# Gate stage of a two-block transformer kernel: gating products on GpSimd, convolution one tile later, attention steps packed earlier

## The reference

```python
h = rmsnorm(x, norm_mix[0])
proj = h @ a_w_in[0]                       # 3 * 768 + 256 columns
gate_b, gate_c, hv, qm = split(proj)       # 768, 768, 768, 256
u = gate_c * hv
y = w_conv[0]*shift(u,2) + w_conv[1]*shift(u,1) + w_conv[2]*u    # causal, 3 taps
main = gate_b * y
mo = memory_attention(qm, mem_n, ...)      # 4 heads of 64 over 256 memory rows
x = x + concat(main, mo) @ w_o[0]
```

## Time and profile before

| | |
|---|---|
| median of 3 runs | 1888.3 us (1887.41 to 1896.14) |
| profiled execution, its own time | 1887.41 us |
| its span in the profile | 1885.6 us |
| PE busy | 1812.6 us, 96% |
| DVE busy | 955.2 us, 51% |
| ACT busy | 751.8 us, 40% |
| POOL busy | 135.2 us, 7% |
| granted TensorE clock, mean | 0.984 |

### The profile page before, as it was taken

One profiled execution on the slowest core, in us unless ns is written; L12 is line 12 of the kernel. 1 busy time (PEld: TensorE's weight loads), 2 busy tenths in 40 slices (PEclk: granted clock), 3 DMA queues, 4 the chain that ended last, 5 costly groups with the idle time before them and its releaser, 6 DMA issues.

```text
span 1885.6 us, 21605 instructions
## 1 busy us (share of the span) xinstructions
PE 1812.6 (96%) x8477; PEld 1482.7 (79%) x8477; DVE 955.2 (51%) x1696; ACT 751.8 (40%) x1475; POOL 135.2 (7%) x169
## 2 busy tenths in 40 slices
PE   7999999999999999999999999998998799999997
PEld 5887888888887777777888888776787688888885
DVE  5666443434344667755443433599944444244345
ACT  6433342323234556645232323423756343232232
POOL 0000010101001111001010101010110000000000
PEclk9999999999999999999999999999998899999999
DMA  6222233333333111123323333222100233333321
GB/s 232 81 68 82 87 93 98 99 99 97 95 101 83 56 56 57 34 58 88 100 91 101 100 91 100 86 73 67 56 1 11 79 100 101 101 90 101 101 90 56
DMA packets 195748, 158.37 MB, mean 84 GB/s; under 512 B 5248, under 2 KB 161152, under 8 KB 195648
## 3 DMA queue, kind: packets, MB, share of 16 engines
q1 hardware_dynamic: 194240, 154.16, 27.2%
q0 software_dynamic: 400, 1.25, 0.3%
q10 hardware_dynamic: 1008, 1.59, 0.2%
HBM read 154.88 MB, written 2.10 MB: 83 GB/s over the span
## 4 chain that ended last, share of the span: by engine, by line
PE 85%; DVE 10%; ACT 3%; issue 1%; DMA 0%; ACTq 0%; DVEq 0%
PE ps L752 28%; PE ps L754 26%; PE ps L753 26%; DVE sb L2261 3%; DVE sb L1856 1%; PE ps L804 1%; PE ps L1184 1%; DVE sb L2387 1%; DVE sb L1870 0%; PE ps L1072 0%; ACT sb L1403 0%; DVE sb L2392 0%; PE ps L1078 0%; ACT sb L1390 0%; DMA sb<-in_con 0%
## 5 line engine op out<-in xcount | busy, mean ns | idle before, releaser
L752 PE MATMUL ps<-sb,sb 128*128 128x512 f32 (+3 forms) x2547 | 990.6, 391 | 20.3 <-DVE sb L1856 7.6
L754 PE MATMUL ps<-sb,sb 128*128 128x512 f32 (+3 forms) x2547 | 968.0, 382 | 0.0
L753 PE MATMUL ps<-sb,sb 128*128 128x512 f32 (+3 forms) x2547 | 967.8, 382 | 0.0
L752 PEld LDWEIGHTS ps<-sb,sb 128*128 128x128 f32 (+1 forms) x2547 | 479.7, 189 | 129.6 <-issue 19.7
L754 PEld LDWEIGHTS ps<-sb,sb 128*128 128x128 f32 (+1 forms) x2547 | 479.5, 189 | 92.4
L753 PEld LDWEIGHTS ps<-sb,sb 128*128 128x128 f32 (+1 forms) x2547 | 480.3, 190 | 85.7
L1856 DVE TENSOR_TENSOR sb<-sb,sb 128x512 fp32r<-128x512 f32 x532 | 351.1, 701 | 351.8 <-ACT sb L1382 351.0
L1382 ACT ACTIVATE sb<-sb 128x512 fp32r<-128x512 f32 x532 | 305.2, 622 | 432.2 <-PE ps L754 432.2
L2065 DVE TENSOR_TENSOR sb<-sb,sb 128x512 fp32r<-128x512 f32 x64 | 68.1, 1063 | 177.0 <-ACT sb L1525 177.0
L650 POOL TENSOR_TENSOR sb<-sb 128x512 f32<-128x512 f32 x64 | 66.9, 1045 | 793.5 <-ACT sb L1535 793.5
L1535 ACT ACTIVATE sb<-ps 128x512 f32<-128x512 f32 x64 | 38.3, 598 | 208.6 <-PE ps L754 208.6
(11 more groups left out here) (204 smaller groups left out, 1031.9 us busy)
## 6 DMA issues: line engine op xcount, KB each, us to landing
sb<-in_w_up SPq DMA_DIRECT2D x86, 512.0 KB, 3.9
sb<-in_w_down SPq DMA_DIRECT2D x86, 512.0 KB, 3.8
sb<-in_w_gate SPq DMA_DIRECT2D x22, 512.0 KB, 3.8
sb<-in_a_w_in SPq DMA_DIRECT2D x20, 512.0 KB, 3.7
sb<-in_w_in SPq DMA_DIRECT2D x20, 512.0 KB, 3.7
sb<-in_w_o SPq DMA_DIRECT2D x16, 512.0 KB, 3.8
sb<-in_w_mem_kv SPq DMA_DIRECT2D x8, 512.0 KB, 7.1
sb<-in_w_out SPq DMA_DIRECT2D x8, 512.0 KB, 3.9
```

What stands on the lines that cost most here:

```text
L752: mm(ps, lh, rh, start=start, stop=False, **k)
L753: mm(ps, lh, rl, start=False, stop=False, **k)
L754: return mm(ps, ll, rh, start=False, stop=stop, **k)
```

## The change

1. `PLAN_A`: the norms of all queries and keys are packed into slots 0 to 3, the turns kt 0 0 and kt 0 1 share slot 2, qt 0 and qt 1 slot 3, qt 2 and qt 3 slot 4; attention starts at slot 5 instead of 7; the second layer's keys have na in slot 29, nb in slot 30, both turns in slot 31, instead of one step a slot in 28 to 33.
2. `RB2`, the square of the spread row norm, goes; a buffer `U2` comes. VectorE's three evictions of a block are now alike: U1, U2 and G are each `ps * RB`.
3. GpSimd makes `U3 = U1 * U2` and `G = G * Y`. VectorE's multiply `Y * RB` goes.
4. The three convolution instructions move on VectorE from behind tile c = 1 to behind tile c = 2 and behind the steps of slot 2n+1.
5. ScalarE and VectorE split the weights of tile n ahead of slot 2n instead of behind it.
6. `gate_hi` waits for GpSimd's product.

```diff
-    PLAN_A[1] += [("na", "q", 0)]
-    PLAN_A[2] += [("nb", "k", 0, 0), ("nb", "k", 0, 1), ("na", "q", 1)]
-    PLAN_A[3] += [("kt", 0, 0), ("nb", "q", 0), ("na", "q", 2)]
-    PLAN_A[4] += [("kt", 0, 1), ("nb", "q", 1), ("na", "q", 3)]
-    PLAN_A[5] += [("qt", 0), ("nb", "q", 2)]
-    PLAN_A[6] += [("qt", 1), ("nb", "q", 3)]
-    attention_steps(PLAN_A, 7, 3)
-    for i in range(2):
-        PLAN_A[9 + 3 * i] += [("qt", 2 + i)]
-        PLAN_A[28 + i] += [("na", "k", 1, i)]
-        PLAN_A[30 + i] += [("nb", "k", 1, i)]
-        PLAN_A[32 + i] += [("kt", 1, i)]
+    PLAN_A[1] += [("nb", "k", 0, 0), ("nb", "k", 0, 1), ("na", "q", 0), ("na", "q", 1)]
+    PLAN_A[2] += [("kt", 0, 0), ("kt", 0, 1), ("nb", "q", 0), ("nb", "q", 1), ("na", "q", 2), ("na", "q", 3)]
+    PLAN_A[3] += [("qt", 0), ("qt", 1), ("nb", "q", 2), ("nb", "q", 3)]
+    PLAN_A[4] += [("qt", 2), ("qt", 3)]
+    attention_steps(PLAN_A, 5, 3)
+    PLAN_A[29] += [("na", "k", 1, 0), ("na", "k", 1, 1)]
+    PLAN_A[30] += [("nb", "k", 1, 0), ("nb", "k", 1, 1)]
+    PLAN_A[31] += [("kt", 1, 0), ("kt", 1, 1)]
...
     def gpsimd_program(e):
+        for j in range(6):
+            z = j % 2
+            q.wait_ge(S("edge"), 1)
+            q.wait_ge(S("gate"), 3 * j + 2)
+            q.wait_ge(S("conv3"), 3 * (j - 1))
+            TTT(U3[:, z, 2:T + 2], U1[:, z, :], U2[:, z, :], ALU.mult).then_inc(S("gate_u3"), 1)
+            q.wait_ge(S("gate"), 3 * j + 3)
+            q.wait_ge(S("conv3"), 3 * j + 3)
+            TTT(G[:, z, :], G[:, z, :], Y[:, z, :], ALU.mult).then_inc(S("gate_out"), 1)
...
-        act(RB2[:, :], banks[7][:, :], ACT.Square).then_inc(S("rb2"), 1)
...
         for n in range(18):
+            weights(SL["gate", n] + 3)
             for s in A.plan[2 * n]:
                 mem_step(A, *s)
-            weights(SL["gate", n] + 3)
...
-            if c == 0:
-                q.wait_ge(S("rb2"), 1)
-                q.wait_ge(S("gate"), 3 * j - 4)
-                tt(U1[:, z, :], ps, RB2[:, :], ALU.mult).then_inc(S("gate"), 1)
-            elif c == 1:
-                q.wait_ge(S("gate"), 3 * j + 1)
-                q.wait_ge(S("conv3"), 4 * (j - 1))
-                tt(U3[:, z, 2:T + 2], ps, U1[:, z, :], ALU.mult).then_inc(S("gate"), 1)
+            if c < 2:
+                q.wait_ge(S("gate_u3"), j - 1)
             else:
-                q.wait_ge(S("conv3"), 4 * j + 3)
-                tt(Y[:, z, :], Y[:, z, :], RB[:, :], ALU.mult).then_inc(S("conv3"), 1)
-                q.wait_ge(S("conv3"), 4 * j + 4)
                 q.wait_ge(S("gate_hi"), j - 1)
-                q.wait_ge(S("gate_lo"), j - 1)
-                tt(G[:, z, :], ps, Y[:, z, :], ALU.mult).then_inc(S("gate"), 1)
+            tt(dst, banks[n % 4][:, :], RB[:, :], ALU.mult).then_inc(S("gate"), 1)
             for s in A.plan[2 * n + 1]:
                 mem_step(A, *s)
             if c == 1 and j > 0:
                 gate_lo(j - 1)
-            if c == 1:
-                q.wait_ge(S("edge"), 1)
-                q.wait_ge(S("gate"), 3 * j + 2)
+            if c == 2:
+                q.wait_ge(S("gate_u3"), j + 1)
+                q.wait_ge(S("gate_out"), j - 1)
                 ts(Y[:, z, :], U3[:, z, 0:T], col("conv3", j), None, ALU.mult).then_inc(S("conv3"), 1)
```

More of the change, by code:

```diff
@@ L483, in build @@
     take = region(x_off)
-    U1, U3, RB2 = take([128, 2, T]), take([128, 2, T + 2]), take([128, T])
+    U1, U2, U3 = take([128, 2, T]), take([128, 2, T]), take([128, 2, T + 2])
     Y, G = take([128, 2, T]), take([128, 2, T])
@@ L1484, in scalar_program @@
         spread(0)
-        act(RB2[:, :], banks[7][:, :], ACT.Square).then_inc(S("rb2"), 1)
         def gate_hi(j):
-            q.wait_ge(S("gate"), 3 * j + 3)
+            q.wait_ge(S("gate_out"), j + 1)
             q.wait_ge(S("w_used"), CH["mem", 1].last + 1)
@@ L1994, in vector_program @@
             j, c, z = n // 3, n % 3, n // 3 % 2
+            weights(SL["gate", n] + 3)
             for s in A.plan[2 * n]:
                 mem_step(A, *s)
-            weights(SL["gate", n] + 3)
-            ps = banks[n % 4][:, :]
+            dst = (U1, U2, G)[c][:, z, :]
             q.wait_ge(S("w_used"), SL["gate", n] + 1)
             q.wait_ge(S("spread"), 1)
-            if c == 0:
-                q.wait_ge(S("rb2"), 1)
-                q.wait_ge(S("gate"), 3 * j - 4)
-                tt(U1[:, z, :], ps, RB2[:, :], ALU.mult).then_inc(S("gate"), 1)
-            elif c == 1:
-                q.wait_ge(S("gate"), 3 * j + 1)
-                q.wait_ge(S("conv3"), 4 * (j - 1))
-                tt(U3[:, z, 2:T + 2], ps, U1[:, z, :], ALU.mult).then_inc(S("gate"), 1)
-            else:
-                q.wait_ge(S("conv3"), 4 * j + 3)
-                tt(Y[:, z, :], Y[:, z, :], RB[:, :], ALU.mult).then_inc(S("conv3"), 1)
-                q.wait_ge(S("conv3"), 4 * j + 4)
+            if c < 2:
+                q.wait_ge(S("gate_u3"), j - 1)
+            else:
                 q.wait_ge(S("gate_hi"), j - 1)
-                q.wait_ge(S("gate_lo"), j - 1)
-                tt(G[:, z, :], ps, Y[:, z, :], ALU.mult).then_inc(S("gate"), 1)
+            tt(dst, banks[n % 4][:, :], RB[:, :], ALU.mult).then_inc(S("gate"), 1)
             for s in A.plan[2 * n + 1]:
@@ L2019, in vector_program @@
                 gate_lo(j - 1)
-            if c == 1:
-                q.wait_ge(S("edge"), 1)
-                q.wait_ge(S("gate"), 3 * j + 2)
+            if c == 2:
+                q.wait_ge(S("gate_u3"), j + 1)
+                q.wait_ge(S("gate_out"), j - 1)
                 ts(Y[:, z, :], U3[:, z, 0:T], col("conv3", j), None, ALU.mult).then_inc(S("conv3"), 1)
                 for k in (1, 2):
-                    q.wait_ge(S("conv3"), 4 * j + k)
+                    q.wait_ge(S("conv3"), 3 * j + k)
                     stt(Y[:, z, :], U3[:, z, k:k + T], col("conv3", 6 * k + j), Y[:, z, :], ALU.mult, ALU.add).then_inc(
```

## The result

The changed kernel takes 1910.5 us (median of 6 runs, 1905.3 to 1915.1) against 1891.1 us (6 runs, 1887.4 to 1896.1): ratio 1.0096, 95% interval 1.0076 to 1.0115, about 1% slower. The direction and the places were forecast, 1902.9 us was too low, and the measured median lies 1.5 us above the range. The changed kernel was timed 15 times in all, these six among them; the median of the 15 is 1908.3 us, just inside the range, so on which side of its upper end the result falls depends on the runs taken. The spread goes with the clock: the mean granted clock is 0.981 where the time is 1905.3 to 1905.9 and 0.975 where it is 1915.1. The profiled execution took 1910.5 us, its span is 1908.7 us, 23.1 longer than before.

The account below looks back on a forecast made before the run. TensorE, busy nearly throughout, was taken as the bound, with at most 2.25 us to gain in the stage. 5.9 + 4.8 + 3.8 - 0.7 + 1.7 = +15.5 on 1887.4 gave 1902.9 us, range 1893.5 to 1909.

Parts of the forecast that it names:

- What bounds the stage: Gate stage: TensorE busy 128.85 of 131.10 us, so at most 2.25 us can be gained, whatever is done for VectorE.
- The rival "not slower": All 432 matmuls of the stage: fewer VectorE multiplies remove small hidden waits, giving back 8.6 us; 1894.3 us, chance 0.07.
- The start, 6.5 in three stalls: Slots 2 to 4: TensorE stalls 2.5, 2.2 and 1.8 us before each pair's second turn; net +5.9 us.
- the bare round trip of 1.23: Two turns through bank 6 with VectorE free: 1.46 us start to start, 0.23 of it the turn, a stall of 1.23.
- The old 0.58: TensorE's wait before the second query turn in the kernel before, 0.58 us, forecast to go.
- The convolution, 0.3 a unit: Before "v": convolution between softmax and "t" stalls TensorE 0.3 us three times and 0.2 for unit 0, 1.1 together.
- GpSimd's hold: GpSimd's product G*Y beside VectorE's weight slab delays it 0.92 us at each of four places, 3.7 together.
- The keys, 3.8: Second layer's keys, slots 29 to 31: TensorE waits for key heads and a round trip, +3.8 us (1.2 to 4.1).
- The projection, -0.7: Before the output projection: Y*RB leaves the front of the last eviction, for which TensorE waits, gaining 0.7 us.
- the clock, 1.7 (0 to 6): Gate stage: half-speed granted clock around the long stalls at the start and key heads costs 1.7 us in all.
- The rival with repeated falls: Clock halves at each of four long stalls, three at the start and slot 31: +19.8 us, 1907.2 us, chance 0.10.
- The base: The forecast was added to the profiled execution's 1887.4 us; the median of the runs shown was 1888.3.

Follow-up runs that it names:

- the version without the faults: The changed kernel with turns one to a slot and the convolution behind the next tile's even slot: 1888.9 us against 1890.0 before the change, ratio 0.9994.
- The filled kernel: The changed kernel with 105 unread matmuls added at nine places where TensorE stalls in the gate stage: 1906.7 us against 1889.6 before the change, ratio 1.0090.
- the repeats: The changed kernel, untouched, profiled two more times: 1905.1 and 1909.8 us.

## Why the prediction was right and where it was wrong

- **What bounds the stage.** Right. TensorE's idle time set all that could be gained, and the version without the faults gained 0.2. The 2.25 is read from stretches that run to 190; the waits inside the stage are 0.58 and 1.56, 2.14 us. The rival "not slower", with small waits taken out of every matmul for 8.6 us, has at most 0.6 us for it: the changed kernel with the old plan has the same sum of brackets as before and a stage 0.6 shorter.
- **The start, 6.5 in three stalls.** Brackets of 2.32, 1.99 and 1.56 against 2.5, 2.2 and 1.8, each 0.15 short of the delay as said above. The chain by pitches held: the old plan had no such waits, one turn a slot left 1.7 (1.0 of it GpSimd's first product, which the prediction took to be hidden), and 1.1 for a pair with VectorE free is the bare round trip of 1.23. The old 0.58 went.
- **The convolution, 0.3 a unit.** Right: 0.26 with GpSimd's product out of the way; and nothing at all with the convolution behind the low half of "t".
- **GpSimd's hold.** Taken as 0.92, measured 1.1 (2.39 to 1.28 or 1.29), within the bound of 1.13. The Trainium skill (SBUF — State Buffer, section Who interferes with whom) has the two engines shut each other out for a whole instruction; the trace comes near it: the hold is 1.1, GpSimd's product alone 1.26, so 0.15 of the product ran beside VectorE. The estimate by that rule, 6.2 for the four places, is above what was measured, 5.4. The four brackets of 1.07, 1.22, 1.23 and 1.24 sum to 4.8. That is the forecast figure only by luck, for the forecast counted whole delays: with 0.15 each for the hidden ends they are the 5.4, 0.6 more, as the hold is 0.2 larger at each.
- **The keys, 3.8.** Brackets of 3.4 in three waits, about 3.8 with the hidden ends. But my reading of its GpSimd part was too simple: taking the product off the slab put it on the norms and kept the wait.
- **The projection, -0.7.** 0.83 for 1.56. The last block's work was hidden: its low half was written at 207.5, 11 us of matmuls into a projection that started at 203.5 want it after 214.
- **The step that failed is the clock, 1.7 (0 to 6).** The stalls came to 14.0 us (12.7 and the hidden ends) against 13.8 forecast. The clock took 6.2, 4.8 and 7.9 us in three executions of the stage. The mechanism was named, its size was off by three to six us, for a reason that I can name: I looked for falls behind the longest idle times and left out those before "v". Behind the 2.3 of the start the clock didn't fall in the first execution; behind 1.22 before "v" it did. The trace of the kernel before had the warning, behind a wait of 1.63 on matmuls of 2 columns (the granted clock is third from the right); another fall began at 1447, behind a wait of 1.34 that ended at 1445.67:

```profile
820.82 1.05 PE L1033 MATMUL ps<-sb,sb 128*128 128x2 f32 x8 [1.63 <-ACT sb L1629]
...
823.00:824.00 1.00, 1.00 (x4) 0.75 (x3) 0.95 (x2) 0.69 (x3) 0.00 (x0) 0.50 0.00 0
```

  Nor does VectorE's lateness hide most of a fall in the start: of the 1.7 that one took at 72 it gave back 0.5 (the third wait, 1.08 for 1.56). The rival with repeated falls, 1907.2, came nearest in time, with falls in other places than it named. The filled kernel, without waits of over 0.6 but for the 0.83 before the projection, and without a fall, shows that the term is real. That the waits cause the falls is likely from it but not proved, since two versions that kept waits of 1.0 to 2.3 had none in their one profiled execution either.
- **The base.** The sum was made on 1887.4, the lowest of the runs; the median of six is 1891.1. With stalls as forecast, that alone would have put the forecast at 1906.6. The range was built from the ends of single terms and centred on the low base, and its upper end, 1909, lies inside the spread of the changed kernel's own runs, 1905.3 to 1915.1. By medians the change costs 19.4 us, against 15.5 forecast.

What stays open: what decides whether the clock falls at a given wait. It was not settled by these runs. In the version with its turns apart five waits of 1.0 to 1.25 passed without a fall, in the one with the convolution behind "t" waits of 2.32, 2.03, 1.54 and 2.28, and some falls elsewhere have no wait before them.

## What to carry to other kernels

A plan written by hand hides its distances: before packing two steps into one slot, ask whether they share a buffer, and what the engine that frees it has queued in front. Where TensorE is busy throughout, work taken off VectorE is worth nothing by itself; moved to GpSimd, here it came back as a hold of 1.0 to 1.1 us on the instruction with two SBUF operands that stood there, whether on 512 elements a partition or on 4. And an idle microsecond of TensorE is to be priced with the clock that may fall behind it: here 12.7 us of waits came with 5 to 8 us more, while 9.0 us of waits in another version came with none.

## What the runs showed of the hardware that I had not expected

In the changed kernel the granted clock fell to half behind a wait of 1.22 us that was followed by twelve matmuls of 64 columns (114.06 to 115.4), and did not behind waits of 2.32 and 1.99 that stood between matmuls of 512 columns in the same execution; in the repeats it fell around the second of these, at 72 and 74. A fall took 1.7 us of matmuls at 115 and at 163, and 2.8 at 187. With 105 useless matmuls in place of the waits the stage was 5.8 us shorter than in the first profile of the changed kernel, and 4.1 and 6.9 shorter than in its repeats.

A GpSimd product of two SBUF operands held a VectorE instruction on 128 x 4 elements for 1.0 us (1.15 in place of 0.16), almost as long as it held up the pair on 128 x 512 (1.1). With the product moved behind the slab, GpSimd ran from 110.27 to 111.55, and the two VectorE instructions of that time, which read one operand from PSUM, took 0.68 (110.02) and 0.69 (110.68), their usual time.
